# Two blocks of a transformer on one core: high and low weight splits, idle products and short steps in a new order

## The chip, the cores and the metric

One core of a Trainium2 chip runs the whole program. The metric is the device time in microseconds from one launch to its end, lower is better; the time of a kernel is the median of its runs.

## What is computed

256 tokens of width 1024 go through a stack of layers, everything in float32. First two blocks with adaptive normalisation, and then two blocks of another kind. Cut to what matters:

```python
def first_block(x, c, ...):                      # DEPTH = 2 layers
    for l in range(DEPTH):
        ada = jax.nn.silu(c) @ w_ada[l] + b_ada[l]
        h = rms_norm(x, norm_mix[l]) * (1.0 + sc_m) + sh_m
        (q_a, kc_a, vc_a, ..., g_a, q_b, k_b, v_b, g_br) = jnp.split(h @ w_in[l], split_at, axis=-1)
        y_a = nsa_mixer(...)                     # compressed, selected and window attention, gated
        y_b = moba_mixer(...)
        gate_a, gate_b = jnp.split(jax.nn.sigmoid(g_br), 2, axis=-1)
        merged = gate_a * (y_a @ w_up_nsa[l]) + gate_b * (y_b @ w_up_moba[l])
        x = x + g_m * (merged @ w_out[l])
        gt, up = jnp.split(h @ w_ffn_in[l], 2, axis=-1)     # h normed again
        x = x + g_f * ((jax.nn.silu(gt) * up) @ w_ffn_out[l])

def second_block(x, mem, ...):
    for layer in range(DEPTH):
        x = x + 0.5 * swiglu(...)                # gate, up, down: 1024 -> 2816 -> 1024
        x = x + (diff_stickbreak_mixer if layer % 2 == 0 else mla_mixer)(...)
        x = x + memory_cross_attention(...)
        x = x + 0.5 * swiglu(...)
```

The differential half of `diff_stickbreak_mixer` subtracts two softmax maps and normalises the heads; its stick-breaking half weighs by products of sigmoids (a cumulative sum of logs).

## The kernel before, in words

**Splits.** A float32 product is made as three products of a high and a low part (high·high, high·low, low·high; `product`, L1462, or `wide_product`, L1468 and L1470, for two of them at once). Weights come by SP's queue in panels of 128 x 2048 (1 MB) into `ring`, which has three slots. ACT copies a panel's high part into `parts` (`split` and `run`, L703), DVE subtracts it from the raw panel and gets the low part (`split` and `tt`, L2222), which also frees the ring's slot for the next DMA. `parts` has two slots: ACT's copy waits until PE has used the panel two before. So each panel goes DMA, ACT, DVE, PE. `splits.until(key, ahead)`, written by hand into each engine's program, says at which place it makes the splits up to the panel `ahead` behind `key`; both programs run strictly in order.

**Programs.** The engines' programs are written out one by one and meet at semaphores. PE's output banks are eight, in pools (`ATT`, `FILL`, `SIDE`, `ROTATING`, `stick`); `open_bank` takes the bank that was opened longest ago and waits until it was freed. `warm(n)` (L1442) issues n products of 256 columns on a zeroed tile that nobody reads: idle products. Before, they stand at the start (12) and behind three of the norms (30 each).

**First mixers.** The columns of `w_in` are made in groups, `ORDER` first; the last groups (4 and 5), the gates and the upward products are "units", two of which are put between the steps of a loop over 24 heads (`HEADS`, `UNITS`; in step i the scores of head i, the turn of head i-2, the output of head i-3). The compressed attention's keys (`kcn`) are turned in step 1, copied by ACT and used in step 2 for 32 products of 16 columns (L1843; the order lists them as 16). DVE makes sums of squares per group (`head_sums`), and masks (L2450) per head. After the loop comes the merged stage: `merged_sum` multiplies gates with the two upward products, `merged_lo` makes the low part for the output product.

**Gated networks** (six): 22 chunks of 128 hidden columns; PE makes gate and up, ACT the silu, DVE the product and the low part, ACT the high part (`hidden hi`). At the end come the down products. In the first two, columns of the next adaptive matrix (L2231, on DVE) are made beside.

**Second blocks.** In the diff mixer, a stick loop of eight heads runs with `kv_beside`, the keys and values of the cross attention, beside it; `between` puts parts of the differential half's normalisation on DVE between its heads; `rsqrts` is ACT's part of the key norms.

## Time and profile before

| | |
|---|---|
| median of 3 runs | 2084.69 us (2081.43 to 2087.8) |
| the profiled execution, its own time | 2091.63 us |
| its span | 2089.8 us |
| mean granted TensorE clock | 0.983 of 2.4 GHz |
| PE busy | 2009.8 us (96%) |
| DVE busy | 1465.0 us (70%) |
| ACT busy | 1090.4 us (52%) |

The profile is of one execution. Its own time is 1.8 us more than its span (launch and end) and 0.33% above the median of the runs. A timeline row gives the start in the span, the length of a group of equal instructions, the engine, the line, what it writes and reads, how many, and in brackets how long the engine stood idle just before and who released it. PE is the matmul engine, DVE the vector engine, ACT the scalar engine. The granted clock of a stretch is a share of 2.4 GHz, so 0.50 is 1.2 GHz.

### The profile page before, as it was taken

What the parts mean: (1) busy time and instruction counts of PE and PEld (TensorE: products, weight loads), DVE (VectorE), ACT (ScalarE), POOL (GpSimd) and SP (SyncE); (2) the same over time, 40 slices, a digit from 0 to 9 for tenths busy, and PEclk for the clock granted to TensorE, in tenths of its full rate; (3) what the DMA queues carried; (4) which work ended last, traced back from release to release, by engine and by line L of the source; (5) the groups of instructions that cost most, each with busy time, mean ns of one, the idle gap of its engine ahead of it and who ended that gap; (6) DMA issues with size and microseconds to landing.
All of it is one profiled execution on the core that took longest, in us unless ns stands there. A gap on an engine that the chain in (4) does not pass through costs nothing. (4 is left out here: it accounts for less than half of the span.)

```text
span 2089.8 us, 31990 instructions
## 1 busy us (share of the span) xinstructions
PE 2009.8 (96%) x12846; PEld 1782.1 (85%) x12846; DVE 1465.0 (70%) x2323; ACT 1090.4 (52%) x1728; POOL 25.7 (1%) x46
## 2 busy tenths in 40 slices
PE   7899899999899899999999998999999999999999
PEld 4779898888789888899889777898898889898888
DVE  6777678877777577647766767677667757767774
ACT  3545544534545455535554655655545546855552
POOL 1001000000001000000000000000000000000000
PEclk9999999999999999999999999999999999999999
DMA  9445448876445357555556432455555554244554
GB/s 316 160 171 198 159 156 279 276 247 215 140 168 187 110 187 230 189 182 182 189 184 208 145 101 101 141 183 183 185 188 190 181 182 152 73 142 142 181 179 144
DMA packets 266211, 372.28 MB, mean 178 GB/s; under 512 B 8400, under 2 KB 160336, under 8 KB 266064
## 3 DMA queue, kind: packets, MB, share of 16 engines
q1 hardware_dynamic: 264736, 368.97, 53.0%
q8 instruction: 102, 1.67, 0.3%
q10 hardware_dynamic: 1328, 1.26, 0.2%
q14 instruction: 45, 0.37, 0.0%
HBM read 369.15 MB, written 1.05 MB: 177 GB/s over the span
## 5 line engine op out<-in xcount | busy, mean ns | idle before, releaser
L2222 DVE TENSOR_TENSOR parts<-ring,parts 128x2048 fp32r<-128x2048 f32 (+2 forms) x304 | 675.5, 2223 | 376.9 <-ACT parts L703 376.4
L703 ACT ACTIVATE parts<-ring 128x2048 fp32r<-128x2048 f32 (+2 forms) x304 | 565.6, 1861 | 592.8 <-PE psum L1470 323.7
L1470 PE MATMUL psum<-h,parts 128*128 128x512 f32 x1920 | 675.1, 396 | 0.0
L1468 PE MATMUL psum<-h,parts 128*128 128x256 f32 x1920 | 539.7, 281 | 2.9 <-DVE parts L2222 2.9
L1470 PEld LDWEIGHTS psum<-h,parts 128*128 128x128 f32 x1920 | 360.3, 188 | 85.9
L1468 PEld LDWEIGHTS psum<-h,parts 128*128 128x128 f32 x1920 | 362.8, 189 | 4.0 <-DVE parts L2222 3.9
L1462 PE MATMUL psum<-h,parts 128*128 128x256 f32 (+1 forms) x2088 | 265.6, 286 | 4.0 <-DVE h L2231 2.0
L1462 PEld LDWEIGHTS psum<-h,parts 128*128 128x128 f32 (+1 forms) x2088 | 255.3, 192 | 6.3 <-issue 3.6
L1462 PE MATMUL psum<-parts,h 128*128 128x512 f32 (+1 forms) x864 | 212.7, 400 | 19.1 <-DVE parts L2222 17.9
L1462 PEld LDWEIGHTS psum<-parts,h 128*128 128x128 f32 x864 | 161.3, 197 | 53.8 <-issue 17.4
L1470 PE MATMUL psum<-hid_hl,parts 128*128 128x512 f32 x528 | 188.2, 400 | 0.0
L1462 PE MATMUL psum<-hid_hl,parts 128*128 128x256 f32 x1584 | 185.0, 279 | 0.8 <-DVE parts L2222 0.8
L1462 PEld LDWEIGHTS psum<-hid_hl,parts 128*128 128x128 f32 x1584 | 183.6, 188 | 2.4 <-DVE parts L2222 2.4
L1468 PE MATMUL psum<-hid_hl,parts 128*128 128x256 f32 x528 | 149.2, 283 | 3.5 <-DVE parts L2222 3.5
L703 ACT ACTIVATE tok<-psum 128x512 f32<-128x512 f32 (+3 forms) x156 | 90.1, 578 | 69.7 <-PE psum L1470 55.7
L1470 PEld LDWEIGHTS psum<-hid_hl,parts 128*128 128x128 f32 x528 | 100.0, 189 | 24.7
L1468 PEld LDWEIGHTS psum<-hid_hl,parts 128*128 128x128 f32 x528 | 99.9, 189 | 3.8 <-DVE parts L2222 3.8
L703 ACT ACTIVATE scores_area<-scores_area,nmax 128x256 f32<-128x256 f32 (+1 forms) x160 | 72.2, 456 | 48.9 <-DVE nmax L2450 48.6
L703 ACT ACTIVATE scores_area<-psum 128x384 f32<-128x384 f32 (+1 forms) x80 | 39.8, 498 | 83.0 <-PE psum L1666 82.8
L2222 DVE TENSOR_TENSOR tok<-psum,tok 128x512 f32<-128x512 f32 x120 | 82.0, 683 | 0.9 <-ACT tok L703 0.7
L1654 PE MATMUL psum<-feat 64*128 64x128 f32 (+4 forms) x320 | 74.2, 353 | 4.3 <-DVE nmax L2450 2.5
L2450 DVE CUSTOM_DVE_ANT_0 scores_area<-psum,const,sums 128x128 f32<-128x128 f32 (+1 forms) x96 | 37.3, 426 | 56.7 <-PE psum L1654 52.9
(255 smaller groups left out, 2118.4 us busy)
## 6 DMA issues: line engine op xcount, KB each, us to landing
ring<-in_w_ada SPq DMA_DIRECT2D x48, 1024.0 KB, 5.4
ring<-in_w_ffn_in SPq DMA_DIRECT2D x88, 512.0 KB, 4.8
ring<-in_ffn_w_gate SPq DMA_DIRECT2D x88, 512.0 KB, 3.7
ring<-in_ffn_w_up SPq DMA_DIRECT2D x88, 512.0 KB, 4.7
ring<-in_w_in SPq DMA_DIRECT2D x36, 1024.0 KB, 4.9
ring<-in_ffn_w_down SPq DMA_DIRECT2D x32, 1024.0 KB, 5.0
ring<-in_w_ffn_out SPq DMA_DIRECT2D x16, 1024.0 KB, 5.0
ring<-in_ffn_w_down SPq DMA_DIRECT2D x16, 768.0 KB, 4.4
```

The lines of the kernel that those rows point to most:

```text
L703: act.activation(out, in_, func, **kw).then_inc(*sig(name, *keys))
L1462: mm = pe.matmul(out, left, right, start=start and n == 0, stop=stop and n == 2, skip_group_check=True)
L1468: pe.matmul(bank[:, 0:S], wt_hl[1], act[:, 0, :], start=start, stop=False, skip_group_check=True)
L1470: return pe.matmul(bank.rearrange("p (a s) -> p a s", a=2), wt_hl[0], act, start=False, stop=stop, skip_group_check=True)
L1654: mm = pe.matmul(b[:, a:c], head["q"][:, P * t:P * t + P], head["k"][:, 0:c - a], start=True, stop=True)
L2222: dve.tensor_tensor(out, a, b, op).then_inc(*sig(name, *keys))
L2450: dve.tensor_tensor_reduce(to, of, add, times, 3.0e38, ALU.add, ALU.min, nmax[:, n % 3, t:t + 1]).then_inc(*sig("dve_nmax", *keys))
```

## The change

It issues 116 more idle products on PE, at ten places, and moves steps on three engines; what is computed stays the same.

```diff
-WARM_NORM, WARM_HEAD, WARM_FIRST = 30, 8, 12
+WARM_NORM, WARM_HEAD, WARM_FIRST = 30, 8, 22
```

ACT, kv_beside (cross keys beside the stick half):

```diff
+                            if g == 1 and n == 0 and k == 2:
+                                rsqrts(normed)
                             yield
                     if g == 0:
-                        rsqrts(squared)
+                        normed = squared
```

ACT, first mixer: gates:

```diff
-                                run(br_gates[:, 0], br_gates[:, 0], ACT.Sigmoid, "act_gates",
-                                    ("gates", l, 0))
                                 run(br_gates[:, 1, 0:4], br_gates[:, 1, 0:4], ACT.Sigmoid,
                                     "act_step")
                                 for q in (6, 7):
...
                                         psum[:, tally.bank(job), :].rearrange(
                                             "p (c s) -> p c s", s=S), ACT.Sigmoid, "act_gates",
                                         ("free", job), *([("gates", l, 1)] if q == 7 else []))
+                                run(br_gates[:, 0], br_gates[:, 0], ACT.Sigmoid, "act_gates",
+                                    ("gates", l, 0))
                                 act.preload_act_table_set(EXP_LN)
```

ACT, first mixer: head loop:

```diff
+                    if i == 2:
+                        copies(("tr kc", l), kc_t)
                     if LAG <= i < HEADS + LAG:
                         m = i - LAG
                         turned_copy(heads[m], base + m)
...
-                    if i == 2:
-                        copies(("tr kc", l), kc_t)
```

ACT, gated networks:

```diff
-                    if i == FC + 1:
-                        splits.until((("up", f), FC // 2 - 1, 1), 3)
                     if i >= 2:
                         act.wait_ge(*at(("product", f, i - 2)))
                         run(hid_hl[:, 0, i - 2, :], piece[:, (i - 2) % 4, :], ACT.Copy,
                             "act_hidden", ("hidden hi", f, i - 2))
+                    if i == FC + 1:
+                        splits.until((("up", f), FC // 2 - 1, 1), 3)
```

PE:

```diff
+            def warm_in(pool, n):
+
+                bank = min(pool, key=lambda b: opened.get(b, -1))
+                if bank in holder:
+                    pe.wait_ge(*at(("free", holder.pop(bank))))
+                opened[bank] = len(tally.banks)
+                warm(n, psum[:, bank, 0:256])
...
+                warm(WARM_HEAD)
                 pe.wait_ge(*at(("copied", key)))
...
                 if l == 0:
                     advance(steps, 3)
                     ada_cols(0, 3, (BANKS + 3,))
+                    advance(steps, 1)
+                    warm_in(ROTATING, 28)
                 whole_of(steps)
...
+                def compressed_scores(g):
+                    pe.wait_ge(*at(("copied", ("tr kc", l))))
+                    b = open_bank(("cmp scores", l, g), SIDE)
+                    for t in range(TT):
+                        for j in range(4):
+                            mm = pe.matmul(b[:, 64 * t + 16 * j:64 * t + 16 * j + 16],
+                                           nq_t[HD * g:HD * g + HD, j, P * t:P * t + P],
+                                           kc_t[HD * g:HD * g + HD, :], start=True, stop=True)
+                    mm.then_inc(*sig("pe_scores", ("full", ("cmp scores", l, g))))
+
                 for i in range(HEADS + LAG + 1):
                     if i < HEADS:
                         scores(i)
                     if LAG <= i < HEADS + LAG:
                         turn(i - LAG)
+                    if i == 23:
+                        next(more, None)
                     if i > LAG:
                         weighted(i - LAG - 1)
-                    for _ in range(UNITS):
+                    for n in range(UNITS - (i == 23)):
                         next(more, None)
+                        if i == 2:
+                            compressed_scores(n)
                     if i == 0:
                         transposes(("tr kw", l), [tok_in[:, t, C_KW:C_KW + P] for t in range(TT)],
                                    [("head", l, "kw", t) for t in range(TT)], (4, 5))
                     if i == 1:
                         transposes(("tr kc", l), [kcn[:].rearrange("p g d -> p (g d)")],
                                    [("kc head", l)], SIDE)
-                    if i == 2:
-                        pe.wait_ge(*at(("copied", ("tr kc", l))))
-                        for g in range(2):
-                            b = open_bank(("cmp scores", l, g), SIDE)
-                            for t in range(TT):
-                                for j in range(4):
-                                    mm = pe.matmul(b[:, 64 * t + 16 * j:64 * t + 16 * j + 16],
-                                                   nq_t[HD * g:HD * g + HD, j, P * t:P * t + P],
-                                                   kc_t[HD * g:HD * g + HD, :], start=True,
-                                                   stop=True)
-                            mm.then_inc(*sig("pe_scores", ("full", ("cmp scores", l, g))))
...
+                warm_in(ATT, 12)
                 more = beside()
...
+                        if n == 7:
+                            warm_in(stick, 6)
                         pe.wait_ge(*at(("weight", n)))
...
                 whole_of(more)
+                warm_in(stick, WARM_HEAD)
                 mixer_out(0, "diff", y_ab, [("y", "stick")])
...
-                        turn_in(0, 1, beside)
+                        turn_in(0, 1, beside, 14)
...
                 for i in range(4 + LAG + 1):
+                    if l == 1 and i == 3:
+                        warm_in(FILL, 6)
                     if i < 4:
                         scores(i)
+                    if l == 1 and i == 1:
+                        warm_in(FILL, WARM_HEAD)
                     if i == 0:
                         q_stats(1)
+                        if l == 1:
+                            warm_in(FILL, WARM_HEAD)
                         advance(more, 2)
```

DVE, first mixers:

```diff
-                    if i < 3:
-                        splits.until((("win", l), i, 1), 2)
+                    splits.until((("win", l), i, 1), 2 if i < 3 else 1)
                     ks = [head_sums(n, HD) for t in range(TT) for _, _, n, _ in per[i]]
...
                 y_lo(("tr y", l, 1, 1), 6, y_mix)
+                splits.until((("w_up_moba", l), 0, 0), 1)
 
                 dve.wait_ge(*at(("gates", l, 1)))
```

DVE, kv_beside and the stick half:

```diff
-                            if g == 1 and n == 0 and k in (0, 2):
-                                xk_head(l, k // 2, ks[k // 2])
+                            if g == 1 and (n, k) in ((0, 3), (1, 1)):
+                                xk_head(l, n, ks[n])
...
-                between = {0: difference, 1: difference_squares, 3: difference_gain,
-                           5: difference_normed}
+                between = {0: difference, 1: difference_squares, 2: difference_gain,
+                           3: lambda: difference_normed(0), 4: lambda: difference_normed(1)}
```

In `transposes`, `idles` idle products go ahead of the wait (the 14 of `turn_in(0, 1, beside, 14)` in the MLA mixer). `difference_normed` is the same code for one of the two token tiles. `warm_in` waits until the pool's oldest bank was freed, writes into it and marks it as just opened.

**Where instructions stand before and after.** On DVE at the start of the first mixer (`parts<-ring,parts` is the low half of a weight panel, `ss<-sq` the head sums, `kcn` the compressed keys, L2450 and L2477 the masks), before:

```order
L2222 TENSOR_TENSOR tok<-tok,rs 128x128
L2339 TENSOR_REDUCE ss<-sq 128x8 x2
L2339 TENSOR_REDUCE ss<-sq 16x2
...
L2222 TENSOR_TENSOR kcn<-kcn,rs 16x128
L2222 TENSOR_TENSOR feat<-psum,const 128x512
L2222 TENSOR_TENSOR parts<-ring,parts 128x2048 x2
L2450 ISA scores_area,nmax<-psum,const 128x128
```

and after:

```order
L2249 TENSOR_TENSOR tok<-tok,rs 128x128
L2249 TENSOR_TENSOR parts<-ring,parts 128x2048
L2366 TENSOR_REDUCE ss<-sq 128x8 x2
L2366 TENSOR_REDUCE ss<-sq 16x2
...
L2249 TENSOR_TENSOR kcn<-kcn,rs 16x128
L2249 TENSOR_TENSOR feat<-psum,const 128x512
L2249 TENSOR_TENSOR parts<-ring,parts 128x2048
L2477 ISA scores_area,nmax<-psum,const 128x128
```

The low half of the first of the two panels now stands ahead of the head sums; the second stays behind the compressed keys.

On DVE in the merged stage (`rot<-aux,psum` and `rot<-rot,feat` are a merged sum, `h<-rot,h` the low part of it), before:

```order
L2222 TENSOR_TENSOR y_mix<-psum,y_mix 128x512
L2222 TENSOR_TENSOR rot<-aux,psum 128x512
L2222 TENSOR_TENSOR rot<-rot,feat 128x512
L2222 TENSOR_TENSOR parts<-ring,parts 128x2048 x2
L2222 TENSOR_TENSOR h<-rot,h 128x512
L2222 TENSOR_TENSOR rot<-aux,psum 128x512
L2222 TENSOR_TENSOR rot<-rot,feat 128x512
```

and after:

```order
L2249 TENSOR_TENSOR y_mix<-psum,y_mix 128x512
L2249 TENSOR_TENSOR parts<-ring,parts 128x2048
L2249 TENSOR_TENSOR rot<-aux,psum 128x512
L2249 TENSOR_TENSOR rot<-rot,feat 128x512
L2249 TENSOR_TENSOR parts<-ring,parts 128x2048
L2249 TENSOR_TENSOR h<-rot,h 128x512
L2249 TENSOR_TENSOR rot<-aux,psum 128x512
```

Again the first of two low halves moved up, ahead of the first merged sum.

On ACT in the stick half (`rs` is the square root for the cross keys' norm, `sq<-psum` and what follows are one head's softplus), the difference:

```order
 L703 ACTIVATE scores_area<-scores_area 128x384
+L703 ACTIVATE sq<-psum 128x384
+L703 ACTIVATE sq<-sq 128x384 x2
+L703 ACTIVATE scores_area<-scores_area 128x384
 L703 ACTIVATE rs<-ss 128x4
 L703 ACTIVATE rs<-rs 128x4
 L703 ACTIVATE rs<-ss 128x4
 L703 ACTIVATE rs<-rs 128x4
-L703 ACTIVATE sq<-psum 128x384
-L703 ACTIVATE sq<-sq 128x384 x2
-L703 ACTIVATE scores_area<-scores_area 128x384
```

The roots moved behind one more head's softplus.

## Rows read from the trace of the kernel before

**Rows 1.** The page, busy time of each engine.

```profile
PE 2009.8 (96%) x12846; PEld 1782.1 (85%) x12846; DVE 1465.0 (70%) x2323; ACT 1090.4 (52%) x1728; POOL 25.7 (1%) x46
```

**Rows 2.** The page, the chain that ended last, shares by engine.

```profile
PE 35%; DVE 3%; ACT 2%; issue 0%; DVEq 0%; ACTq 0%
```

**Rows 3.** Windows: PE, PEld, DVE, ACT, POOL busy (instructions), granted clock, DMA share, GB/s.

```profile
27.50:30.90 3.40, 3.40 (x6) 0.49 (x5) 2.71 (x6) 1.49 (x3) 0.00 (x0) 0.50 1.06 404
...
99.10:106.00 6.90, 5.10 (x12) 4.02 (x13) 3.86 (x2) 0.07 (x1) 0.00 (x0) 0.51 0.62 214
119.60:123.00 3.40, 3.40 (x10) 2.63 (x9) 0.97 (x3) 1.20 (x5) 0.00 (x0) 0.50 0.65 246
...
443.90:447.30 3.40, 3.40 (x12) 2.92 (x11) 2.38 (x3) 0.00 (x0) 0.00 (x0) 0.50 1.02 374
...
1174.30:1177.80 3.50, 3.50 (x10) 2.39 (x8) 2.69 (x2) 1.77 (x6) 0.00 (x0) 0.51 0.68 255
...
1280.20:1287.00 6.80, 5.60 (x26) 5.63 (x27) 2.44 (x2) 1.08 (x2) 0.00 (x0) 0.50 0.43 151
1785.30:1792.10 6.80, 5.94 (x25) 5.62 (x26) 6.36 (x14) 5.79 (x14) 0.00 (x0) 0.50 0.13 32
```

**Rows 4.** Timeline of PE, start of the first mixer: start us, us, engine line op.

```profile
100.90 5.33 PE L1462 MATMUL psum<-parts,h 128*128 128x512 f32 x12 [5.89 <-DVE parts L2222]
...
107.23 3.02 PE L1462 MATMUL psum<-parts,h 128*128 128x512 f32 x12
...
114.44 3.32 PE L1843 MATMUL psum<-feat 64*128 64x16 f32 x32
```

**Rows 5.** Timeline of DVE, the same stretch.

```profile
93.95 0.69 DVE L2339 TENSOR_REDUCE ss<-sq 128x8 f32<-128x512 f32 x1 [6.96 <-ACT sq L703]
...
98.49 4.47 DVE L2222 TENSOR_TENSOR parts<-ring,parts 128x2048 fp32r<-128x2048 f32 x2
```

**Rows 6.** Timeline of ACT, the same stretch.

```profile
86.47 1.92 ACT L703 ACTIVATE parts<-ring 128x2048 fp32r<-128x2048 f32 x1 [0.45 <-PE psum L1462]
```

**Rows 7.** Timeline of PE, merged stage of the first mixer.

```profile
251.39 5.90 PE L1462 MATMUL psum<-y_mix,parts 128*128 128x256 f32 x48
260.48 8.56 PE L1462 MATMUL psum<-y_mix,parts 128*128 128x256 f32 x48 [3.19 <-DVE parts L2222]
```

**Rows 8.** Timeline of DVE, the same stretch.

```profile
256.72 0.69 DVE L2222 TENSOR_TENSOR rot<-aux,psum 128x512 f32<-128x512 f32 x1 [3.73 <-PE psum L1462]
...
258.05 4.49 DVE L2222 TENSOR_TENSOR parts<-ring,parts 128x2048 fp32r<-128x2048 f32 x2
```

**Rows 9.** Timeline of PE, end of the first gated network's chunks.

```profile
442.91 0.39 PE L1468 MATMUL psum<-hid_hl,parts 128*128 128x256 f32 x1 [3.49 <-DVE parts L2222]
```

**Rows 10.** Timeline of DVE, the same stretch.

```profile
437.01 0.43 DVE L2222 TENSOR_TENSOR hid_hl<-rot,hid_hl 128x256 fp32r<-128x256 f32 x1 [3.60 <-ACT hid_hl L703]
437.54 3.11 DVE L2231 SCALAR_TENSOR_TENSOR tok<-ring,scol,tok 128x512 f32<-128x512 f32 x4
440.57 4.49 DVE L2222 TENSOR_TENSOR parts<-ring,parts 128x2048 fp32r<-128x2048 f32 x2
```

**Rows 11.** Timeline of ACT, stick half.

```profile
1256.49 0.21 ACT L703 ACTIVATE rs<-ss 128x4 f32<-128x4 f32 x1 [5.12 <-DVE ss L2339]
```

**Rows 12.** Timeline of PE, end of the stick half.

```profile
1260.93 0.67 PE L2022 MATMUL psum<-rot,const 128*128 128x256 f32 x2 [2.66 <-DVE rot L2222]
...
1281.40 5.46 PE L1462 MATMUL psum<-y_ab,parts 128*128 128x256 f32 x24 [1.22 <-ACT y L703]
```

**Rows 13.** Timeline of PE, idle products of an existing warm-up.

```profile
294.48 3.44 PE L1442 MATMUL psum<-idle 128*128 128x256 bf16 x30
```

**Rows 14.** Timeline of PE, three other holes.

```profile
47.41 2.92 PE L1462 MATMUL psum<-parts,h 128*128 128x512 f32 x7 [4.08 <-DVE parts L2222]
...
228.36 1.07 PE L1679 MATMUL psum<-tok,scores_area 128*128 128x64 f32 x6 [1.98 <-DVE y_mix L2222]
...
1172.57 0.89 PE L1654 MATMUL psum<-feat 64*128 64x128 f32 x4 [1.41 <-ACT tok L703]
```

More of the change, by code:

```diff
@@ L1618, in plain_out, with transposes @@
                     warm(WARM_NORM if then[0] != "cross" else 0)
-            def transposes(job, inputs, ready=(), pool=ROTATING):
+            def transposes(job, inputs, ready=(), pool=ROTATING, idles=0):
                 b = open_bank(job, pool)
+                warm(idles, b[:, 0:256])
                 for key in ready:
@@ L2062, in up_kv, with turn_in @@
                                         (lambda k: ("h", "latk", 4 + k)) if i == 0 else None, pool=pool)
-                def turn_in(a, g, pool):
+                def turn_in(a, g, pool, idles=0):
                     src = (tok_mq, tok_mk)[a]
@@ L2069, in turn_in @@
                                     for t in range(TT)],
-                                   [("mla head", a, g)], pool)
+                                   [("mla head", a, g)], pool, idles * (j == 0))
                 steps = up_q(0)
@@ L3032, in difference_gain, with difference_normed @@
                         stt(one, one, 1.0 - LAMBDA_INIT, gain, ALU.mult, ALU.mult)
-                def difference_normed():
-                    for t, (one, two) in enumerate(maps):
-                        dve.wait_ge(*at(("subln rs", t)))
-                        settle()
-                        ts(wt[:, t, 20:24], wt[:, t, 20:24], -0.5 / P, -0.5 * EPS, ALU.mult, ALU.add)
-                        settle()
-                        refine(wt[:, t, 16:20], wt[:, t, 20:24], wt[:, t, 24:28])
-                        tt(one, one, over(wt[:, t, 16:20], 4, P), ALU.mult, "dve_y",
-                           *([("y", "diff normed")] if t else []))
+                def difference_normed(t):
+                    one, two = maps[t]
+                    dve.wait_ge(*at(("subln rs", t)))
+                    settle()
+                    ts(wt[:, t, 20:24], wt[:, t, 20:24], -0.5 / P, -0.5 * EPS, ALU.mult, ALU.add)
+                    settle()
+                    refine(wt[:, t, 16:20], wt[:, t, 20:24], wt[:, t, 24:28])
+                    tt(one, one, over(wt[:, t, 16:20], 4, P), ALU.mult, "dve_y",
+                       *([("y", "diff normed")] if t else []))
                 strict = con("strict")
```

## The prediction

> **What bounds the kernel now.** I read five views in this order: busy time, the chain that ended last, the granted clock, the PE timeline at its holes, and the other engines' rows at those holes. PE works 96% of the span [rows 1], so about 80 us of its 2089.8 are idle. The chain says the same: PE 35%, DVE 3%, ACT 2% [rows 2]; time comes only from PE's holes or from PE's own speed. PE's speed is the second store: the mean granted clock is 0.983, which over 2089.8 us is 35.5 us lost. The windows show that it is lost in short stretches at exactly half clock, 1.2 in place of 2.4 GHz, some 3.4 us or 6.8 us long; in each PE stays nearly fully busy, so a stretch costs half its length, 1.7 or 3.4 us [rows 3]. There are fourteen of them. I put each beside the timeline: nearly all begin at or just behind a hole, or behind products with few columns. So a hole is paid twice, once as idle time and once in slow products. The change works on both: it moves work of DVE and ACT so that holes close, and fills other holes with idle products.
>
> **Start of the first block's mixers (two layers).** PE stands still for 5.89 us until DVE has made the low half of a weight panel, and the 12 products behind it take 5.33 us, against 3.02 for the same 12 products at full clock [rows 4]. DVE made that panel, with the next, in 4.47 us from 98.49, yet it had sat idle for 6.96 us until 93.95 [rows 5]. ACT had made the high half by 88.39 [rows 6]. The change puts the low half of this panel ahead of the last head sums, into that idle time: 88.4 to 90.6, with 3.3 us of margin before the head sums. Gain 5.89 + 2.31 = 8.2. What is late next: the products go on with the second panel only after 24 products, and its low half comes behind the compressed keys at about 100.7, earlier than PE then asks (about 103); but the masks of the second step now queue behind it on DVE, and the copy of the compressed keys moves ahead of other ACT work. I take 1.0 for these together: 7.2 each, 14.4 in all (ends 0 and 16.4). The DMA issue of a following panel waits for this low half too and goes some 10 us earlier; a transfer more in flight has no reader behind it here, so nothing.
>
> **Compressed scores in two halves.** The 32 products of 16 columns take 3.32 us [rows 4], and 119.60 to 123.00 runs at half clock behind them [rows 3]. The change puts 12 products of 512 columns between their halves. The same work is issued; a gain comes only if the clock holds, 1.7 per layer at most. I take half the two: 1.5 (ends 0 and 3.4).
>
> **Merged stage (two layers).** 48 products take 5.90 at full clock and then 8.56 behind a hole of 3.19 [rows 7]: 3.19 + 2.66 = 5.85. DVE was idle 3.73 us, then took two products' sums (0.69 each) and the two low halves, 4.49 [rows 8]. The change makes the first of them in that idle time. Late next: once PE is done early, DVE still has two merged sums of two 0.69 us operations each and one low half of 2.25, about 5 us, while PE has some 30 products in hand before it needs them, 3.7 us at the 5.90 for 48 of [rows 7]. New wait about 1.3 to 1.5. So 4.3 each, 8.6 (ends 0 and 11.7).
>
> **Gated networks.** In the first one PE waits 3.49 us for a low half [rows 9] and then runs at half clock [rows 3]. DVE had waited 3.60 us for ACT's copy of the last hidden chunk, and did the adaptive columns (3.11) and the low halves (4.49 for two, PE needs the first) behind it [rows 10]; ACT had put a 1.92 us high half ahead of the copy, itself late by its DMA. Now the copy is first. DVE is done 3.6 earlier, just when PE asks: 3.49 + 1.7 - 0.2 = 5.0 (ends 1 and 5.5). The other five networks have no such hole. There a high half moves behind a 0.4 us copy and nothing waits: nothing, unless the copy's own input is late (rival 5).
>
> **Stick half.** ACT stood 5.12 us before square roots for the cross keys while softplus work was queued behind them [rows 11]; PE's wait of 2.66 comes of it, other waits of the DVE chain, head by head, of the normalisation packed into one step, and at the end PE waits 1.22 and makes 24 products in 5.46 [rows 12], where 48 at full clock in 5.90 [rows 7] make it 2.95. With the roots one head later and the normalisation spread over two steps, I follow the DVE chain (five 0.56 us operations a head) and get the output products 3.6 earlier; 2.5 more from the clock [rows 3]: 6.1 (ends 1 and 8.5).
>
> **Idle products.** 30 of them take 3.44 us, 0.115 each [rows 13]. At the very start 10 + 8 + 8 + 28 lie in holes of which the largest is 4.08 [rows 14]; about 0.9 of them sticks out, and two stretches at half clock (one is 27.50 to 30.90) may go: 3.4 - 0.9 = 2.5 (ends -0.9 and 3.4). Ahead of the diff mixer, 12 stand behind the hole of 1.41, not in it [rows 14], because they wait for the same release as the scores did: +1.4, against 1.7 from the clock: 0.3 (ends -1.4 and 0.3). In MLA 14 of them (1.6) stand in a hole, and the stretch 1785.30 to 1792.10 may go [rows 3]; a DVE low half holds PE soon after, so 1.4 (ends -0.5 and 3.4). In the second cross attention there is no slow stretch: -0.3. **Step 23** of the head loop has a unit ahead of a product that waited 1.98 [rows 14]: 1.0 in one layer, nothing in the other, where ACT's copy is what is late.
>
> **A page's rule against this.** The slow stretch at 119.60 follows PE work without a hole [rows 3, 4], and those from 1174.30 and 1280.20 [rows 3] follow holes of only 1.41 and 1.22 [rows 12, 14]. The Trainium skill, TensorE: Matmul & The Clock Gate, section Why this matters for your kernels, holds that it is long idle gaps between bursts that take the clock down. By it the slow stretches at short holes have no such cause and fillers there buy nothing (rival 4); these rows speak against it.
>
> **Sum.** 14.4 + 1.5 + 8.6 + 5.0 + 6.1 + 2.5 + 0.3 + 1.4 - 0.3 + 1.0 = 40.5. From it I take 2.5 for slow stretches that come at new places: with the phase of everything shifted, one or two of 1.7 are likely. That leaves 38. The profiled execution took 2091.6 and would become 2053.6; the median of the runs before is 2084.7, 0.33% lower, so I forecast **2047 us**.
>
> **Rivals.** *(1) The forecast*, 0.53; its own range is 2039 to 2054.
> *(2) The next wait takes the place of the one removed.* DVE is busy 70%, and behind each moved panel it has the same total work. If half of the waits I count as gone (9.8 + 3.4 + 3.3 + 3.6 + 1.0 = 21.1) come back a few steps on, the gain is 38 - 10.5: 2057. For: both mixer loops run DVE and PE close together. Against: DVE had 7 us idle just ahead. 0.23.
> *(3) The clock falls all the same.* Then only waits are gained, and idle products cost: 21.1 - 0.9 - 1.4 - 0.3 = 18.5, so 2066. For: slow stretches stand in places where PE was busy, so what brings them isn't a hole alone. Against: where a large hole goes, all that stood around the slow stretch goes. 0.10.
> *(4) Only the large holes bring the clock down.* The stretches at busy PE work and at holes under 2 us stay, with other causes: 38 less the clock terms 1.5 (halves), 2.5 (stick end), 1.7 (start), 1.7 (diff) and 1.9 (MLA, whose idle products then cost 0.5) is 28.7, so 2056. This is what the page's rule comes to here. For: the two long stretches of the merged stages do follow holes of 3.19 [rows 7]. Against: the rows named above. 0.08.
> *(5) Slower.* ACT runs in order. In all six networks its high half now waits behind the copy of the last hidden chunk, and so for DVE's product of that chunk. If that product stood behind the adaptive columns and two low halves (3.11 + 4.49 [rows 10]), each network would pay up to 7.6, 46 in all: 38 gained, 8 lost, 2093. It decides from 7.3 us each. Against: DVE was idle for 3.60 us just there [rows 10], so the product was ready; these networks have no hole now. 0.03. Between it and the others, 0.03 for no change.
>
> **Range and chances.** A measurement of this kernel can tell about 0.3%, 6 us, from no change. Only rival (5) lies above 2078. The lower end: all clock terms full and no new slow stretch, 38 + 2.5 + 1.9 + 3.3 = 46 gives 2039; the clock of one run against another moves some us, so 2038. The upper end reaches to rival (3), 2066.
>
> **What would show it.** Right: no PE hole above 2 us at about 95 and 550, none before the second half of the moba products, none before the down products of the first network; mean clock near 0.99; span about 2053. Rival 2: DVE-released waits of 1 to 4 us one to three steps on. Rival 3: mean clock still 0.983 with fewer holes. Rival 4: 0.983 exceeded only by the stretches at the large holes, slow ones left at 1174 and 1280. Rival 5: a new PE wait of several us in every network, released by DVE behind ACT's high half. The term I trust least is the clock at the stick end and the network; the one that would hurt most is the mixer start.

## The result and the profile after

| | before | after |
|---|---|---|
| median | 2084.78 us (2081.43 to 2087.8, 4 runs) | 2063.21 us (2058.53 to 2066.29, 4 runs) |
| ratio | 1 | 0.9887, 95% interval 0.9868 to 0.9907 |
| span of the profiled execution | 2089.8 us | 2064.5 us |
| mean granted clock, profiled execution | 0.983 | 0.991 |

The change makes the kernel 21.6 us faster, by 1.1%. The forecast was 38 us and 2047: the measured time lies in the whole range (2038 to 2066), near its upper end, and outside the forecast's own range of 2039 to 2054. Two lines of the page of after, busy time and the chain:

```profile
PE 2010.7 (97%) x12962; PEld 1783.9 (86%) x12962; DVE 1465.0 (71%) x2323; ACT 1091.0 (53%) x1728; POOL 26.0 (1%) x46
...
PE 36%; DVE 3%; ACT 2%; issue 0%; DVEq 0%; ACTq 0%
```

PE does the same work (2009.8 us busy before, 2010.7 with 116 more idle products) in a span 25.3 us shorter. The windows of after at all places where its clock was low (columns as in [rows 3]):

```profile
109.70:113.10 3.40, 3.40 (x11) 2.74 (x10) 1.32 (x6) 1.55 (x6) 0.00 (x0) 0.51 0.97 368
225.80:229.20 3.40, 3.40 (x19) 3.40 (x18) 0.00 (x0) 3.37 (x3) 0.00 (x0) 0.50 0.88 297
263.30:266.70 3.40, 3.40 (x19) 3.40 (x18) 1.70 (x1) 0.00 (x0) 0.00 (x0) 0.51 0.90 278
553.50:567.10 13.60, 13.60 (x46) 11.04 (x45) 5.01 (x13) 2.02 (x7) 0.00 (x0) 0.50 0.45 154
710.50:713.90 3.40, 3.23 (x15) 3.25 (x16) 2.92 (x3) 0.00 (x0) 0.00 (x0) 0.50 0.88 266
1150.80:1154.20 3.40, 3.22 (x14) 2.20 (x15) 0.00 (x0) 2.50 (x3) 0.00 (x0) 0.50 0.65 202
1239.50:1246.40 6.90, 6.04 (x19) 5.29 (x20) 6.67 (x13) 1.67 (x4) 0.00 (x0) 0.51 0.10 39
```

Half of these 37 us is lost, 18.6; before it was 35.5. All seven are at 1.2 GHz. The stretch in the MLA mixer, those at 27 and 48 us and the one behind the first gated network are gone, as forecast; the longest, 553.50 to 567.10, is new in this length, and PE is busy in all 13.6 us of it.

The PE timeline at the start of the first mixer, which answers to [rows 4]:

```profile
92.46 3.06 PE L1472 MATMUL psum<-parts,h 128*128 128x512 f32 x12
...
102.78 1.96 PE L1841 MATMUL psum<-feat 64*128 64x16 f32 x16 [0.36 <-ACT feat L703]
104.67 1.66 PE L1472 MATMUL psum<-parts,h 128*128 128x512 f32 x6
106.26 1.96 PE L1841 MATMUL psum<-feat 64*128 64x16 f32 x16
108.06 0.90 PE L1665 MATMUL psum<-feat 64*128 64x128 f32 x4
...
109.99 4.48 PE L1472 MATMUL psum<-parts,h 128*128 128x512 f32 x12
...
131.74 0.67 PE L1878 MATMUL psum<-feat 128*128 128x512 f32 x1 [1.88 <-ACT feat L703]
```

The hole of 5.89 us is gone without a rest: the products follow the scores at once. Step 3's scores begin at 108.06; before they began at 117.61. But the two halves of the compressed scores take 1.96 each where the block took 3.32, a wait of 0.36 for the copied keys is ahead of the first, and the clock falls behind them as before (12 products in 4.48). A later wait for the compressed values has grown from 0.84 to 1.88 (the last row; 1.06 in a second profile of the same kernel, experiment 9). DVE, answering to [rows 5]:

```profile
85.92 2.29 DVE L2249 TENSOR_TENSOR parts<-ring,parts 128x2048 fp32r<-128x2048 f32 x1 [1.46 <-ACT parts L703]
91.46 0.69 DVE L2366 TENSOR_REDUCE ss<-sq 128x8 f32<-128x512 f32 x1 [3.25 <-ACT sq L703]
```

The low half lies in the idle time, 3.25 us of which are left. The merged stage on PE and DVE, answering to [rows 7, 8]:

```profile
242.62 11.55 PE L1472 MATMUL psum<-y_mix,parts 128*128 128x256 f32 x96
254.00 5.91 PE L1472 MATMUL psum<-h,parts 128*128 128x256 f32 x48
262.15 6.03 PE L1472 MATMUL psum<-h,parts 128*128 128x256 f32 x36 [2.24 <-DVE h L2249]
```

```profile
256.28 0.68 DVE L2249 TENSOR_TENSOR rot<-aux,psum 128x512 f32<-128x512 f32 x1
...
258.93 2.28 DVE L2249 TENSOR_TENSOR parts<-ring,parts 128x2048 fp32r<-128x2048 f32 x1
261.31 1.49 DVE L2249 TENSOR_TENSOR h<-rot,h 128x512 fp32r<-128x512 f32 x2
```

All 96 products run through at full clock, but the output products wait 2.24 us: a low half of 2.28 stands in DVE's order ahead of the low part that PE waits for. Three more places on PE: the gates, the idle products ahead of the diff mixer, and the stick half ([rows 12, 14]):

```profile
219.86 0.85 PE L1690 MATMUL psum<-tok,scores_area 128*128 128x64 f32 x6 [0.56 <-DVE y_mix L2249]
...
225.12 4.59 PE L1472 MATMUL psum<-y_mix,parts 128*128 128x256 f32 x24 [1.97 <-ACT aux L703]
...
1150.98 2.74 PE L1444 MATMUL psum<-idle 128*128 128x256 bf16 x12 [1.32 <-ACT tok L703]
...
1240.37 1.19 PE L2040 MATMUL psum<-rot,const 128*128 128x256 f32 x2 [2.28 <-DVE rot L2249]
...
1256.75 0.88 PE L2055 MATMUL psum<-tok,scores_area 128*128 128x64 f32 x6 [1.28 <-DVE scores_area L2249]
...
1260.24 2.00 PE L1472 MATMUL psum<-y_ab,parts 128*128 128x256 f32 x15 [0.35 <-ACT y L703]
```

**Where the time went.** DVE makes the same 304 low halves in the same order in both traces, so their starts are marks: how much earlier the same one comes in after, taken where DVE follows PE closely. Each row is what a place added to that lead. The last column is the same from the second profile of the changed kernel (experiment 9), against the same profile of before.

| place | forecast | first profile | second profile |
|---|---|---|---|
| start, to 57 us | 2.5 | 2.5 | 2.5 |
| first mixer's start with the compressed scores | 7.2 + 0.75 | 6.0 (7.0, of which 1.0 is given back at 131.74) | 5.3 |
| its gates and merged stage | 1.0 + 4.3 | 2.4 | 4.5 |
| first gated network | 5.0 | 4.9 | 5.3 |
| second mixer's start with the compressed scores | 7.2 + 0.75 | 1.8 | 3.3 |
| its merged stage | 4.3 | 2.2 | 0.6 |
| gated networks, 770 to 1100 us | 0 | 1.6 | 1.6 |
| 1100 us to the diff mixer's first heads | 0.3 | -1.2 | -0.8 |
| stick half | 6.1 | 3.4 | 3.2 |
| MLA mixer | 1.4 | 1.4 | 1.4 |
| second cross attention | -0.3 | 0.2 | 0.1 |

Single places differ by up to 2 us between two executions of the same kernel, so a row is good to about that. Part of it is the one execution of before, which was slower than the median: the profiled executions of experiments 6 and 7 are 4.7 and 7.3 us shorter, while their medians are 0.3 and 3.0 us under the kernel before. The 1.6 of the gated networks stands in these two as well, at 1.6 and 1.0, though nothing was changed there.

### The profile page after: what moved, and what is told of

It reads as the page before. It is cut to its first block and busy times, and to the rows that moved or that the text cites. A ratio compares the mean times of both kernels' runs of the same rounds, so it can differ in the third digit from the quotient of the medians.

```text
span 2064.5 us, 32220 instructions
## 1 busy us (share of the span) xinstructions
PE 2010.7 (97%) x12962; PEld 1783.9 (86%) x12962; DVE 1465.0 (71%) x2323; ACT 1091.0 (53%) x1728; POOL 26.0 (1%) x46
## 5 line engine op out<-in xcount | busy, mean ns | idle before, releaser
L1472 PE MATMUL psum<-parts,h 128*128 128x512 f32 (+1 forms) x864 | 207.6, 392 | 4.2 <-DVE parts L2249 3.1
L2477 DVE CUSTOM_DVE_ANT_0 scores_area<-psum,const,sums 128x128 f32<-128x128 f32 (+1 forms) x96 | 37.3, 426 | 57.2 <-PE psum L1665 53.4
```

The lines of the kernel that those rows point to most:

```text
L1472: mm = pe.matmul(out, left, right, start=start and n == 0, stop=stop and n == 2, skip_group_check=True)
L2477: dve.tensor_tensor_reduce(to, of, add, times, 3.0e38, ALU.add, ALU.min, nmax[:, n % 3, t:t + 1]).then_inc(*sig("dve_nmax", *keys))
```

## The experiments

Two columns stand with each kernel's time below. "Clock" is the mean over its runs of span x (1 - granted clock), what half clock takes; "rest" is span x clock. The clock is given to three digits, so one run's figure is good to 1 us, and idle time within a slow stretch is counted under the clock though the low clock costs nothing there. Ratios are to the kernel before on the same chip.

| kernel | median us (runs) | ratio (95%) | clock | rest |
|---|---|---|---|---|
| before | 2086.8 (29) | 1 | 31.1 | 2054.1 |
| changed | 2063.2 (4) | 0.9887 (0.9868 to 0.9907) | 14.4 | 2046.6 |
| changed, again | 2063.0 (4) | 0.9878 (0.9863 to 0.9892) | 12.4 | 2048.7 |
| no idle products | 2064.0 (4) | 0.9904 (0.9890 to 0.9918) | 20.6 | 2041.4 |
| before + early low halves | 2073.7 (6) | 0.9938 (0.9918 to 0.9958) | 25.5 | 2043.6 |
| scores together | 2058.2 (4) | 0.9875 (0.9859 to 0.9892) | 13.4 | 2042.7 |
| scores filled | 2069.7 (6) | 0.9927 (0.9911 to 0.9942) | 16.2 | 2051.0 |
| before + hidden copy first | 2080.9 (10) | 0.9972 (0.9957 to 0.9986) | 27.0 | 2053.0 |
| before + stick order | 2086.5 (12) | 1.0003 (0.9992 to 1.0015) | 32.5 | 2052.5 |
| before + start's idle products | 2083.8 (11) | 0.9981 (0.9972 to 0.9990) | 25.4 | 2055.9 |
| recombined | 2054.4 (4) | 0.9847 (0.9830 to 0.9864) | 11.3 | 2041.4 |
| recombined, no idle products | 2061.4 (4) | 0.9863 (0.9847 to 0.9879) | 17.0 | 2041.8 |
| recombined, idle ones at the start only | 2059.3 (4) | 0.9867 (0.9848 to 0.9885) | 18.0 | 2040.8 |
| recombined, gates as before | 2055.5 (4) | 0.9842 (0.9827 to 0.9856) | 12.3 | 2041.3 |

The kernel before was measured at 2084.5 (experiments 1 to 4), 2086.8 (5 to 8) and 2088.0 (9 to 12), so medians of different rounds compare less well than their ratios do.

**1. The idle products taken out.**

```diff
-WARM_NORM, WARM_HEAD, WARM_FIRST = 30, 8, 22
+WARM_NORM, WARM_HEAD, WARM_FIRST = 30, 8, 12
...
-                warm_in(ATT, 12)
```

(and every other added `warm` and `warm_in`.)

> The changed kernel without any of the 116 added idle products; all moved steps stay. Theory A (idle products hold the clock at the start and in the MLA mixer, cost 1.3 us ahead of the diff mixer): slower than the changed kernel by 2 to 5 us, about 2066 to 2068, the start alone 2.5 us slower by the splits' times (two stretches at half clock come back within the first 60 us, and one at the MLA loop). Theory B (fillers in holes of under 2 us buy nothing and cost their own time): faster than the changed kernel by 1 to 3 us, about 2061, no slow stretch more than there are now except the one behind the hole of 4.08 us.

2064.0 against 2063.2: neither theory; the difference is within the spread. The clock takes 6.2 us more and the rest 5.2 less, so what the 116 products hold, they also cost. Place by place its profile is 2.2 us behind at 57 us (a stretch at 47 is back); ahead of the diff mixer it has a second slow stretch, 1.7, and yet comes out level, since the 12 idle products are off the path. How the other part of the 5.2 is spread isn't settled; some of it is idle time that is counted under the clock.

**2. The early low halves alone.**

```diff
-                    if i < 3:
-                        splits.until((("win", l), i, 1), 2)
+                    splits.until((("win", l), i, 1), 2 if i < 3 else 1)
...
+                splits.until((("w_up_moba", l), 0, 0), 1)
```

> The kernel before with nothing but the two low halves on DVE moved up (start of the mixers, merged stage). Theory A: both holes of 5.89 us and both of 3.19 us go; 2.2 us of a new wait comes in front of each output product; compressed scores stay in one block and the clock falls behind them as before. 2 x (5.9 + 2.3) + 2 x (3.2 - 2.2 + 1.7) = 21.8 less what new slow stretches take: 8 to 20 us faster, 2065 to 2077, most of the whole change's gain. Theory B (the low halves alone only move the wait to the copy of the compressed keys and to the masks): under 6 us faster.

2073.7, 11 us faster, as theory A has it; half of the whole gain from two lines. The prediction had 23.0 for them (7.2 and 4.3 in each of two layers), 13.2 of waiting and 9.9 of clock. By the means of the runs they gave 13.5: 9.8 of rest and 3.7 of clock (the kernel before had 2053.4 and 29.2 in that round). The rest is lower than the changed kernel's. Four of the six runs are at 2073 to 2075, the profiled one at 2062.0 with a clock of 0.993: the clock's part varies from 14.4 to 33.2 us among them, more than the time does.

**3. The compressed scores in one block.**

```diff
-                        if i == 2:
-                            compressed_scores(n)
+                    if i == 2:
+                        compressed_scores(0)
+                        compressed_scores(1)
```

> The changed kernel with the two halves of the compressed scores in one block again, behind both units; ACT's order stays as changed. Theory A (the 32 products of 16 columns load the array little and bring the clock down, halves make it no better): within 4 us of the changed kernel, a slow stretch of 3 to 7 us right behind or in the block in both layers, and not the 13 us of the second layer. Theory B (halves do hold the clock in one layer): slower by 2 to 6 us. The waits of 0.36 us before the scores go, since the copy has longer.

2058.2 against 2063.2 by the medians; the intervals of the ratios overlap, so the medians alone don't settle it. The trace does for its part: PE in that kernel, first mixer.

```profile
102.57 3.02 PE L1472 MATMUL psum<-parts,h 128*128 128x512 f32 x12
105.51 3.32 PE L1841 MATMUL psum<-feat 64*128 64x16 f32 x32
108.69 0.90 PE L1665 MATMUL psum<-feat 64*128 64x128 f32 x4
```

From step 2's first product to step 3's scores it takes 6.12 us; in the changed kernel 7.28 (100.78 to 108.06), all at full clock. The halves cost 1.16 us a layer: 0.36 is waiting, and 0.8 comes of the two breaks more, since each half has its own start and end (1.96 + 1.96 against 3.32, 0.60 by durations, and neighbours overlap less). And a slow stretch follows all the same (from 109.8, one in each layer).

**4. Idle products among the narrow ones.**

```diff
+                            if j % 2:
+                                warm(2, b[:, 256:512])
```

> The changed kernel with 8 idle products of 256 columns in each half of the compressed scores (two behind every second narrow product), 32 in all. They cost 0.11 us each, 0.9 per half, 3.5 in all. Theory A (narrow products bring the clock down): the slow stretches at 110 and at 553 to 567 go, 1.7 + 6.8 = 8.5 us back, so 2 to 5 us faster than the changed kernel in executions that had them. Theory B (the stretches there have another cause): 3.5 us slower, stretches stay.

2069.7, 6.5 us slower: theory B's side. The fillers cost more than the 0.9 us per half that was expected: a half with them takes 3.2 us in place of 1.96 (103.58 to 106.80 in its trace). Its profile has a slow stretch of 6.8 us behind the scores in both layers. The fillers didn't hold the clock, so theory A's reading of the cause (only little work in PE brings it down) isn't borne out, or fillers of this kind don't count for it. Ten profiles were taken of kernels with the mixers' hole closed, so there are 20 such places: in 19 of them the clock falls at or just behind these scores (from 104 to 112 us, and from 552 to 563). In the four profiles with the hole open it fell at the hole all eight times, and at the scores four. The place is certain, the cause is open.

**5. The last hidden copy first.**

```diff
-                    if i == FC + 1:
-                        splits.until((("up", f), FC // 2 - 1, 1), 3)
                     if i >= 2:
...
+                    if i == FC + 1:
+                        splits.until((("up", f), FC // 2 - 1, 1), 3)
```

> The kernel before with nothing but ACT's copy of the last hidden chunk ahead of the high half, in all six networks. Theory A: the hole of 3.49 us ahead of the down products of the first network goes, with one stretch at half clock; nothing elsewhere: 3 to 5 us faster, about 2080, and the low halves' times shift by -3.1 to -5 at that place alone. Rival: the high half comes late in the other five networks: waits of 0.3 us or more that are not there now, no gain or a loss.

2080.9 against 2086.8, 0.28%: theory A. In the profiles the lead grows by 5.0 us at that place: the wait of 3.49 and the slow stretch of 3.4 us behind it, 1.7, are gone. The second isn't certainly the edit's: in the profiles of experiments 2 and 6, which lack it, the hole was 2.60 and no slow stretch followed either. PE has no wait of 0.3 us or more in any network that it didn't have. That settles rival 5 of the prediction.

**6. The stick half's order alone.**

```diff
+                            if g == 1 and n == 0 and k == 2:
+                                rsqrts(normed)
...
-                        rsqrts(squared)
+                        normed = squared
...
-                between = {0: difference, 1: difference_squares, 3: difference_gain,
-                           5: difference_normed}
+                between = {0: difference, 1: difference_squares, 2: difference_gain,
+                           3: lambda: difference_normed(0), 4: lambda: difference_normed(1)}
```

> The kernel before with nothing but the new order of the stick half (ACT's roots one head later, DVE's key heads and the differential half's normalisation spread). Theory A: the waits on this chain fall from 2.66 + 1.80 + 0.93 to 2.28 + 1.28, and the last 1.22 stays: 2.0 to 3.5 us less waiting, and the clock falls once or twice in this stretch as before: 2 to 4 us faster, about 2081. Rival (the forecast's term): 6 us faster, because the slow stretch at the output products goes too.

Ratio 1.0003: no gain is left in the time. The profile shows one, 3.0 us at that place, of which 1.7 is one slow stretch less and 1.3 the rest; its waits of 0.3 us or more add up to 6.2 where they were 7.95. The largest waits left are these:

```profile
1258.67 0.67 PE L2024 MATMUL psum<-rot,const 128*128 128x256 f32 x2 [2.29 <-DVE rot L2224]
...
1272.27 0.88 PE L2037 MATMUL psum<-tok,scores_area 128*128 128x64 f32 x6 [1.27 <-DVE scores_area L2224]
...
1275.76 5.46 PE L1464 MATMUL psum<-y_ab,parts 128*128 128x256 f32 x24 [1.22 <-ACT y L703]
```

The last row is that of [rows 12]: 1.22 us of waiting and 24 products in 5.46, so the clock is low at the output products just the same. Over 12 runs the rest is 1.6 us lower, as the waits say, and the clock takes 1.4 more. Why it does so isn't shown.

**7. The start's idle products alone.**

```diff
-WARM_NORM, WARM_HEAD, WARM_FIRST = 30, 8, 12
+WARM_NORM, WARM_HEAD, WARM_FIRST = 30, 8, 22
...
+                warm(WARM_HEAD)
                 pe.wait_ge(*at(("copied", key)))
...
+                    warm_in(ROTATING, 28)
```

> The kernel before with nothing but the idle products at the start (22, 8, 8 and 28). Theory A: no stretch at half clock in the first 60 us where there were two, 0.9 us of the idle products on the path: 2.5 us faster in the profile's first 60 us, 1 to 3 us in the median, about 2082 to 2083. Rival (fillers buy nothing): 0.9 us slower, 2085 to 2086.

2083.8 against 2086.8, 0.19% with an interval clear of 1: theory A. The clock takes 5.7 us less, the rest is 1.8 more; no slow stretch stands in its profile's first 60 us.

**8. Recombined.** The scores in one block, no idle products ahead of the diff mixer and in the cross attention, and DVE's merged stage in another order:

```diff
                 merged_sum(2)
-                merged_sum(3)
                 splits.until((("w_up_moba", l), 1, 0), 2)
                 merged_lo(2)
+                merged_sum(3)
                 merged_lo(3)
```

> The changed kernel with the compressed scores in one block, no idle products ahead of the diff mixer and in the second cross attention, and in the merged stage DVE's second output panel and low part ahead of the last merged sum. Theory A: against the changed kernel 2.3 us for the block, 1.3 for the diff start, 0.3 for the cross attention, 2 x 1.5 for the wait of 2.24 us ahead of the output products: 7 us and what the clock gives: about 2055, under both kernels. Rival: the clock falls at other places in exchange, as it did between the kernels so far: 2058 to 2062.

2054.4, theory A's time, under both kernels: 8.8 us under the changed one by the medians. In one round, a near twin of it (experiment 12) took 2054.8 to 2056.0 where the changed kernel took 2060.8 to 2064.9. The wait in the merged stage, and where the clock still falls:

```profile
253.85 5.91 PE L1472 MATMUL psum<-h,parts 128*128 128x256 f32 x48
260.68 14.51 PE L1472 MATMUL psum<-h,parts 128*128 128x256 f32 x116 [0.92 <-DVE h L2243]
```

```profile
106.60:113.30 6.70, 6.70 (x25) 5.57 (x25) 3.64 (x11) 1.71 (x6) 0.00 (x0) 0.50 0.90 311
226.10:229.40 3.30, 3.30 (x18) 3.30 (x17) 0.00 (x0) 3.27 (x3) 0.00 (x0) 0.50 0.88 312
553.80:557.00 3.20, 3.20 (x13) 2.81 (x12) 1.98 (x11) 1.77 (x6) 0.00 (x0) 0.50 1.04 398
673.20:676.50 3.30, 3.30 (x18) 3.30 (x17) 1.34 (x2) 0.00 (x0) 0.00 (x0) 0.50 0.44 84
1144.30:1147.60 3.30, 3.30 (x9) 2.62 (x9) 2.65 (x5) 2.65 (x6) 0.00 (x0) 0.50 0.92 307
1233.00:1236.30 3.30, 3.30 (x10) 2.63 (x10) 3.27 (x5) 0.00 (x0) 0.00 (x0) 0.50 0.02 5
```

PE's wait of 2.24 us has become 0.92, in both layers. Six stretches are left, and PE is busy all through each of them. Four follow a wait of 1.4 to 2.3 us; ahead of those at 106.60 and 553.80 there is none of 0.35 or more for 15 us.

**9. The changed kernel again**, unchanged.

> The changed kernel, nothing else, on the same chip as the three that follow and with a second profile. Theory A (what a stretch at half clock hits varies from execution to execution): the median stays at 2061 to 2065, the holes stay the same to 0.1 us, but the 13.6 us at half clock from 553 us on need not be there; two to four slow stretches are in other places. Rival (the halves bring that run of four down each time): 13 us at half clock at the same place again.

2063.0: the median stays. In both first blocks' mixers and merged stages the waits are the same to 0.1 us, but for two: that at 131.74 is 1.06 now, and one of 0.68 has come at 231. The slow stretches of the two mixers' starts:

```profile
104.90:108.20 3.30, 3.30 (x10) 2.27 (x9) 3.12 (x3) 0.00 (x0) 0.00 (x0) 0.50 0.36 74
111.80:115.00 3.20, 3.20 (x9) 2.52 (x8) 0.81 (x2) 1.01 (x5) 0.00 (x0) 0.50 0.34 124
552.10:562.20 10.10, 10.10 (x38) 8.32 (x37) 4.76 (x12) 1.67 (x6) 0.00 (x0) 0.50 0.61 208
```

10.1 us in one piece at 552 where there were 13.6, so the rival is nearer. It isn't so each time: in the profile of experiment 1, which has the halves too, the clock fell for 10.2 us in the first layer and not at all in the second. In the three profiles with halves and no fillers, three of the six places have 10 us or more; in the six profiles with one block, none of the twelve has more than 6.8. At 1.2 GHz 16 of the narrow products take 3.60 us in place of 1.96 (trace of the changed kernel). That the halves are why a fall lasts is likely by these counts, and not shown.

**10 and 11. Recombined without idle products, and with the start's alone.** The edits are those of experiment 1 on the recombined kernel, wholly and for the stick half and the MLA mixer alone.

> The recombined kernel (scores in one block, no idle products ahead of the diff mixer and in the cross attention, second output panel earlier) without any of the added idle products at all. Theory A (those at the start and in the MLA mixer hold the clock): 3 to 5 us slower than the recombined kernel, 2058 to 2060, with slow stretches at 47 us and at the MLA loop. Rival: as fast as it, 2053 to 2056, because the idle products' own time is as long as what the clock gives.

> The recombined kernel with the idle products at the start alone (not in the stick half and the MLA mixer). Theory A: the MLA stretch at half clock comes back (1.4 us slower there), the stick end loses its idle products without cost: 1 to 3 us slower than the recombined kernel. Rival: no difference, the start is all that they bring.

2061.4 and 2059.3 against 2054.4: 5 to 7 us by medians of two rounds, 3.3 and 4.1 by the ratios, whose intervals overlap. The surer comparison is with experiment 12, in their own round, which has these idle products: its four runs took 2054.8 to 2056.0, those of experiments 10 and 11 2056.9 to 2062.8 and 2058.1 to 2065.9. So here the idle products are worth some 4 to 6 us, and it is clock: 17.0 and 18.0 against 12.3, with the same rest. That is theory A of the first, but for one of its signs: the slow stretch in the MLA mixer came back in neither profile. The start's alone brought nothing sure. How the clock's gain divides among the places isn't settled.

**12. The gates as before.**

```diff
-                    if i == 23:
-                        next(more, None)
...
-                    for n in range(UNITS - (i == 23)):
+                    for n in range(UNITS):
```

(and the sigmoid of the first gates back in its place on ACT.)

> The recombined kernel with the sigmoid of the gates and PE's units in step 23 as in the kernel before. Theory A (the waits only change places there, 2.79 to 2.53 and 2.21 to 1.94 us): within 1.5 us of the recombined kernel, holes of 1.98 and 0.81 us in the first mixer and 2.21 us in the second back, and those of 1.97 and 1.52 us gone. Rival (the forecast's term): 1 us or more slower, and a slow stretch more, since the larger waits stand closer together.

2055.5 against 2054.4, within the runs' spread. The waits are 1.98 and 2.33 in the first mixer and 2.21 in the second; in the recombined kernel they are 0.56 and 1.97, and 0.42 and 1.54. They mostly change places; 1.8 and 0.3 us less of them in the profiles are 1.1 us in the medians, which no interval here tells from nothing.

## Why the prediction was right, and where its sizes failed

Right: the direction, the bound (PE's waits and its clock), and the largest term, the mixers' start. The hole there went to nothing by the move that was named, the start gave 2.5 of 2.5, the first network 4.9 of 5.0. That PE is the bound rests on its busy time alone; the shares of the chain in [rows 2] add up to only 40% of the span.

Wrong: the size. The gain was 21.6 of 38. The time lies outside the forecast's own range, between rival 2 (2057) and rival 3 (2066); it is in the whole range because that reaches up to rival 3. Rival 5 is out (experiment 5), and so is rival 3, since the clock takes 15 to 17 us less (14.4 against 29.2 in the first round and 31.1 in the second). Rival 2's mechanism, waits that come back, is part of why. Rival 4 has the compressed scores and the diff mixer right, where the first profile shows nothing gained from the clock, and the start wrong: there the idle products took 5.7 us off the clock's part (experiment 7). The step that failed most is the price of the two early low halves, 23.0 us, which gave 11 to 13.5 alone (experiment 2). As far as rest and clock tell them apart, the waiting came to three quarters of its forecast and the clock to a third: no longer low at the holes, it fell again a few us on.

**Mixers' starts: the term for the clock.** "Gain 5.89 + 2.31" held in both layers for the wait. But before, the clock was low at the hole (6.8 us) and once more behind the scores (3.4); after, 3.4 us in the first layer and 13.6 in the second, and 6.5 and 10.1 in the second profile. I had taken 2.5 us for slow stretches at new places, one or two of 1.7; the second layer's alone took 6.8. How long it lasts there changes from one execution to the next, so the 6.1 us missing in the second layer are partly chance.

**Compressed scores in halves, forecast 1.5 gained: 2.3 lost.** "The same work is issued" left out what a break costs. Two halves take 0.60 more than one block, with 0.36 of waiting for a copy that the block didn't have to wait for, and they don't hold the clock (experiments 3, 4 and 9).

**Merged stage, some 4 short in two layers.** The new wait was named but sized 1.3 to 1.5; it is 2.24. The "about 5 us" of DVE left out the low part itself, which PE waits for: from the first of the two sums (256.28) to its end (262.05) it is 5.8. That is 0.8 a layer; the other 1 or so is the clock, which I took as fully won: it fell again at the new wait (263.30 and 710.50), for 3.4 us where it had been 6.8. Experiment 8 takes 1.3 of the wait away by DVE's order alone. The gates' 1.0 was none: 1.98 + 0.81 became 0.56 + 1.97 in the first mixer. That is rival 2's mechanism.

**Diff mixer, 1.5 short.** The 12 idle products stood behind the wait as forecast, with their 1.3 us, but the clock fell in them: they run 2.74 us at 1.2 GHz. The lower end of that term (-1.4) was nearer. In the second profile the clock held there, and the place still gave -0.8.

**Stick half, 2.7 short.** The waits give about 1.8 of the 3.6 (7.95 to 6.18 in experiment 6): 2.28 and 1.28 are left. The clock gives 1.7 of the 2.5: the slow stretch at the output products went, but one of 6.8 us stands at a head before them, and in experiment 6 it stayed at the products.

**MLA mixer, 1.4 of 1.4, may be luck.** The slow stretch there is missing in all six profiles with the 14 idle products, but in four of the eight without them too; experiment 7's profile has none of them and gained the same 1.4 at this place. No run tests them alone.

**The rule of the page.** The Trainium skill, TensorE: Matmul & The Clock Gate, section Why this matters for your kernels, names long idle gaps between bursts as what brings the clock down. For long waits the traces here agree: after their first 30 us the fourteen profiles have 24 waits of PE of 3.19 to 5.89 us, and the clock is low at all 24, in the wait or within 1.5 us of its end; of the six of 2.60 to 2.66 it is so at three. But it also falls without such a gap: of the six slow stretches of the recombined kernel none holds idle time of PE, the longest wait ahead of any is 2.3 us, and two have none. So the rule explains the large terms of the prediction and not what was left over.

## What to carry to other kernels

Look at DVE's or ACT's idle time just ahead of a PE wait and move the operation PE waits for into it: two such lines gave half of this gain, and for the wait that comes next, count the whole of that engine's work up to the operation PE needs, that operation included, and look at its order: what PE needs goes first. Idle products belong in front of a wait that isn't their own; behind it they cost their time, and may run at half clock themselves. Don't count on cutting a block of narrow products in two to hold the clock: here it cost 1.2 us each time; a term for the clock is the least certain one of a sum, so give it a range to either side, and read its effect from several runs' clocks. One profile of each kernel isn't enough to say which place gained: two profiles of one kernel differed by 2 us at single places here.

## What the runs showed of the hardware

- A block of 16 narrow fp32 products (16 columns) takes 1.96 us and one of 32 takes 3.32 at full clock (traces of the changed kernel and of experiment 3): 0.085 us for each product more, and 0.6 for the break.
- The clock falls to 1.2 GHz with PE busy without a break: 6.70 of 6.70 us from 106.60 in the recombined kernel, 13.60 of 13.60 from 553.50 in the changed one. Eight idle products among each 16 narrow ones didn't prevent it (experiment 4, 6.8 us in both layers).
- At each of the 24 waits of PE of 3.19 to 5.89 us in the fourteen profiles (after the first 30 us) the clock was low, in the wait or within 1.5 us of its end; of the 31 waits of 2.2 to 2.5 us, at 15.
- Runs of one kernel differ mainly by clock: the early low halves alone took 2061.97 us at 0.993 and 2074.93 at 0.984. Their span x clock differs by 6 us the other way; over the runs of one kernel it has a standard deviation of 0.8 to 2.4 us.
